# Prompt attention: VectorE's low half before the take in short tiles, early products in the last slot of their step

## What is computed

```
s = einsum('bqhd,bkhd->bhqk', q, K) * scale
s = s + F_q[..., None] - F_k
s = where(k_pos <= q_pos, s, -inf)
p = softmax(s)
o = einsum('bhqk,bkhd->bqhd', p, V)
b = o * silu(gate)
```

## Time and profile before

| what | value |
|---|---|
| median of 3 executions | 1475.28 us (1474.33 to 1477.14) |
| the profiled execution, its own time | 1475.86 us |
| its span | 1474.1 us |
| instructions | 24037 |
| PE (TensorE matmul) | 1439.7 us busy, 98% |
| DVE (VectorE) | 859.8 us, 58% |
| ACT (ScalarE) | 623.1 us, 42% |
| POOL (GpSimd) | 531.6 us, 36% |
| granted TensorE clock | 1.0 of full speed, mean |
| prompt attention, on TensorE | about 727 to 1158 us from the span's start |

### The profile page before, as it was taken

The page is one execution under the profiler, slowest core; times in us unless marked ns, Lnnn a source line. Parts: engine busy times, 40 slices in busy tenths (PEclk is TensorE's granted clock), DMA queues, the critical chain, the costliest instruction groups (busy, mean ns, idle before and its releaser), DMA issues.

```text
span 1474.1 us, 24037 instructions
## 1 busy us (share of the span) xinstructions
PE 1439.7 (98%) x8896; PEld 1299.1 (88%) x8896; DVE 859.8 (58%) x1858; ACT 623.1 (42%) x1324; POOL 531.6 (36%) x819
## 2 busy tenths in 40 slices
PE   8999999999999999999999999999999899999998
PEld 8998888888889999999988898898898799987887
DVE  4333103343355362232498898889889688798663
ACT  5434012131131110110287787788778555532220
POOL 2110003545541011010346655655655686502221
PEclk9999999999999999999999999999999999999999
DMA  5533114544232020044257536536624498635442
GB/s 166 150 126 102 46 59 129 161 129 136 87 95 62 22 72 25 12 98 94 57 97 149 110 72 140 126 64 129 132 47 138 150 329 271 235 130 185 133 160 93
DMA packets 179620, 173.95 MB, mean 118 GB/s; under 512 B 72431, under 2 KB 137872, under 8 KB 176432
## 3 DMA queue, kind: packets, MB, share of 16 engines
q1 hardware_dynamic: 176992, 163.44, 40.0%
q10 hardware_dynamic: 2448, 8.91, 1.5%
q0 software_dynamic: 64, 0.07, 0.1%
HBM read 123.27 MB, written 49.12 MB: 117 GB/s over the span
## 4 chain that ended last, share of the span: by engine, by line
PE 60%; DVE 16%; issue 11%; POOL 7%; ACT 4%; DMA 2%; SPq 0%; DVEq 0%; POOLq 0%; ACTq 0%
PE banks L1065 18%; PE banks L1059 14%; PE banks L2800 7%; DVE pa_s_ring L1589 7%; POOL in_h_rstd L586 4%; PE banks L1657 3%; POOL in_out L591 3%; PE banks L2232 3%; PE banks L1673 3%; PE banks L1674 2%; PE banks L2211 2%; PE banks L2268 2%; DVE in_out L872 2%; DVE pa_pt_lo L1618 1%; PE banks L1648 1%
## 5 line engine op out<-in xcount | busy, mean ns | idle before, releaser
L1059 PE MATMUL banks<-in_w_hi,in_xt_hi 128*128 128x512 f32 (+1 forms) x680 | 242.8, 357 | 1.5 <-ACT in_out L637 1.1
L1059 PE MATMUL banks<-in_w_hi,in_xt_lo 128*128 128x512 f32 (+1 forms) x680 | 237.8, 350 | 0.0
L1059 PE MATMUL banks<-in_w_lo,in_xt_hi 128*128 128x512 f32 (+1 forms) x680 | 237.2, 349 | 0.0
L1618 DVE TENSOR_TENSOR pa_pt_lo<-banks,pa_pt_hi 128x512 fp32r<-128x512 f32 (+2 forms) x320 | 192.7, 606 | 20.6 <-ACT pa_pt_hi L1560 19.6
L1065 PE MATMUL banks<-in_xt_hi,in_w_hi 128*128 128x384 f32 (+1 forms) x576 | 192.4, 334 | 0.9 <-DVE in_w_lo L770 0.7
L1065 PE MATMUL banks<-in_xt_hi,in_w_lo 128*128 128x384 f32 (+1 forms) x576 | 189.3, 329 | 0.0
L1065 PE MATMUL banks<-in_xt_lo,in_w_hi 128*128 128x384 f32 (+1 forms) x576 | 189.0, 328 | 0.0
L1536 ACT ACTIVATE pa_s_ring<-pa_s_ring,pa_low 128x1024 f32<-128x1024 f32 (+2 forms) x192 | 172.9, 901 | 27.4 <-DVE pa_low L1589 25.8
L1560 ACT ACTIVATE pa_pt_hi<-banks 128x512 fp32r<-128x512 f32 (+2 forms) x320 | 162.0, 530 | 51.9 <-PE banks L1657 50.1
L1657 PE MATMUL banks<-ident,pa_s_ring 128*128 128x128 f32 x1088 | 172.3, 274 | 8.1 <-DVE pa_pt_lo L1618 7.4
L1673 PE MATMUL banks<-pa_pt_hi,pa_vs 128*128 128x256 f32 x576 | 166.1, 304 | 6.4 <-DVE pa_parts L1600 6.0
(11 more groups left out here) (309 smaller groups left out, 2887.8 us busy)
## 6 DMA issues: line engine op xcount, KB each, us to landing
sa_k_c<-in_cache_k_dram SPq DMA_DIRECT2D x8, 2048.0 KB, 10.6
sa_v_c<-in_cache_v_dram SPq DMA_DIRECT2D x28, 512.0 KB, 5.3
out_dram<-in_out SPq DMA_DIRECT2D x34, 256.0 KB, 2.1
out_dram<-op_x ACTq DMA_DIRECT2D x17, 512.0 KB, 3.3
scratch_qk_t<-in_t_hi SPq DMA_DIRECT2D x32, 256.0 KB, 2.6
scratch_qk_t<-in_t_lo SPq DMA_DIRECT2D x32, 256.0 KB, 3.0
pa_q_l<-scratch_qk_t SPq DMA_DIRECT2D x16, 512.0 KB, 13.0
pa_ks<-scratch_qk_t SPq DMA_DIRECT2D x16, 512.0 KB, 6.5
```

Source lines behind the costliest of these rows:

```text
L1059: mm = pe.matmul(ps[:, u % NBANK, 0:n], tile_of(xa, t)[:, k, :], wa[:, k, c0:c0 + n], start=(k == 0 and q == 0), stop=(k == KT - 1 and q = ...
L1618: dve.tensor_tensor(pt_lo[g % 2][:, b:b + nb, cols], ps_t[:, turn_use(h, j, n) % 3, 0:nb * P].rearrange("p (b q) -> p b q", q=P), pt_hi[g ...
```

## The change

On VectorE, in steps whose tile has a single quad (j = 0 to 3), the low half of tile j now stands ahead of the take of tile j + 3's first quad. On TensorE, for 2 <= j < 8 (BLK = 8), all blocks of products of a step are multiplied in its last slot, after that slot's turn and scores, and no longer spread over the slots. Everything else is as it was.

```diff
@@ -1608,7 +1608,7 @@
                 n_take = len(quads(nxt[1])) if nxt else 0
                 slots = max(len(banks), n_take)
                 for n in range(slots):
-                    if n < n_take:
+                    if n < n_take and len(banks) > 1:
                         take_chunk(*nxt, n)
                     if n < len(banks):
                         b, nb = banks[n]
@@ -1619,6 +1619,8 @@
                                           ps_t[:, turn_use(h, j, n) % 3, 0:nb * P].rearrange("p (b q) -> p b q", q=P),
                                           pt_hi[g % 2][:, b:b + nb, cols].bitcast(F32),
                                           ALU.subtract).then_inc(lo_done, 1)
+                    if n < n_take and len(banks) == 1:
+                        take_chunk(*nxt, n)
                     if n == min(1, slots - 1) and j % 2 == 1:
                         ended = pair_ended(h, j - 1, LAG)
                         if ended:
@@ -1705,7 +1707,9 @@
                         done = pair_ended(h, j - 1, LAG)
                         if done:
                             turn_output(*done)
-                    if ended:
+                    if ended and 2 <= j < BLK:
+                        values(*ended, ours if n == slots - 1 else [])
+                    elif ended:
                         values(*ended, ours[len(ours) * n // slots:len(ours) * (n + 1) // slots])
         turn_output(H - 1, NG - 2)
         following("queries")
```

## The result

The changed kernel takes 1478.61 us (median of 20 runs, 1476.46 to 1480.34) against 1474.93 us before (median of 20). Two of the 20 executions before, 1565.61 and 3509.92 us, lie far outside the others, and the ratio leaves them out. It is 1.0022, 95% interval 1.0015 to 1.0028: slower by 0.22%, some 3.3 us (the two medians are 3.7 us apart). The interval leaves out 1, but the difference is hardly more than the 3 us that the forecast took as no change. The profiled execution took 1477.82 us, its span is 1476.1 us.

A forecast was written before the change was run, and what follows sets the result against it. VectorE, almost gapless within a head, was taken to bound the prompt attention. +0.6 us in heads 1 to 7 and +0.2 us in head 0 made +0.8 us: 1476.1 us forecast, range 1473.2 to 1478.9 us.

The forecast's parts named there:

- What bounds a head: From step 2 VectorE works almost without a gap; TensorE's waits in steps 2 to 7 are its shadow.
- Late start (a): Step 2 of heads 1 to 7 begins with tile 2's low half, waiting for ACT's high half: +0.12 us on the path.
- Neighbouring takes (b): Steps 2 and 3: second take directly behind the first, losing overlap; +0.115 us each, +0.23 us a head, bounds nothing to 0.17 each.
- the signs for right: Low half 0.12 us late, gap near 0.03 us, tile 8's wait gone, TensorE's waits shifted, head 53.2 to 53.3 us.
- (c): Step 3's low half would find its input ready and not wait, with only 0.05 us to spare.
- The take-back: Tile 8's scores end earlier, so VectorE recovers its 0.19 us wait and 0.08 us overlap: at most -0.27 us a head.
- The sum: Heads 1 to 7: 0.12 + 0.23 - 0.27 = +0.08 us each; head 0 +0.2 us; together +0.8 us.
- The case: Whole kernel: time within about 0.2%, 3 us, of no change; chance 0.83, faster 0.07, slower 0.10.
- Rival A: TensorE's waits in steps 4 and 6 are lost time and vanish: -10.4 us, 1464.9 us; chance 0.06.
- B: Neighbouring takes cost nothing; heads 1 to 7 gain 0.15 us each, 1474.2 us; chance 0.16.
- C: Postponed products hold up step 5 and tile 8's scores, nothing comes back; 0.46 us a head, 1478.9 us; chance 0.09.
- The waits forecast for TensorE: Step 4's wait shrinks below 0.6 us, step 6's goes, step 8's grows from 0.23 to about 0.9 us.

The follow-up runs named there:

- e2: Kernel before with only the products of steps 4 to 7 moved to the last slot, VectorE's order as before; 1473.12 us, ratio 0.9984.
- e7: Changed kernel with the gating of steps 1 and 3 between the two takes instead of behind them; 1475.55 us, 1.0003 of the kernel before.
- e6: e2 with ScalarE's copy of an output (even steps) behind the second high half of its step; 1464.92 us, 0.9925 of the kernel before.
- e1: Changed kernel with products spread over the slots as before, so only VectorE's order differs; 1480.51 us, 1.0036 of the kernel before.
- e3: Changed kernel where second takes of tiles 4 to 6 neither wait for nor read the first take's minimum; 1473.62 us, 0.9988 of the kernel before.
- e5: Changed kernel with the low half ahead of the first take in steps 4 to 7 too; 1484.14 us, 1.0055 of the kernel before.
- e4: Changed kernel where second takes of tiles 4 to 6 still wait but start from a constant; 1477.18 us, 1.0010 of the kernel before.

## Why the prediction was right or wrong

- **What bounds a head** held: VectorE, with ScalarE at some places, from the low half or take of step 2 to the late steps. e2 (TensorE's waits moved, 0.4 us a head and not 1.3), e7 (its wait removed, nothing gained) and e6 (VectorE's waits for ScalarE shortened, 0.95 us a head on top of e2) show it from three sides.
- **Late start (a)** held: +0.12 us, in e1 one part of 0.64.
- **Neighbouring takes (b)** is the step that failed, in size: the term of +0.23 us a head was 0.52 us. The forecast took 0.115 us each from two dependent additions with a gap of 0.03 us, and named 0.17 us as the upper bound from handoffs between engines. Measured is a gap of 0.18 us, so 0.26 us each, beyond the bound. The price was read from a pair whose second instruction carries its wait itself, while a second take has a wait instruction of its own ahead of it (0.10 us already in the pair one row higher, at 1310.83), two semaphores in it, and a read-out to wait for. e1, e3 and e5 show the price; what share of it each of the three has is read from rows alone. The line for wrong, a head over 53.5 us, was just not crossed by heads 1 and 3 to 6 (53.48 to 53.50), but the signs for right, a gap near 0.03 us and a head of 53.2 to 53.3 us, were missed.
- **(c)** held, but by luck: the low half of step 3 did not wait in the changed kernel, where the larger gap of (b) had put it at 893.34. In e3, where the takes overlap, it waited, by 0.15 us with the lost overlap. With a gap as small as the forecast's it would have had next to no margin.
- **The take-back** held as a mechanism and was somewhat larger, 0.38 for 0.27 us.
- **The sum**: 0.12 + 0.52 - 0.38 = 0.26 us a head against 0.28 measured (53.48 to 53.50 for 53.19 to 53.24), and head 0 3 x 0.26 - 0.15 = 0.63 us, measured 0.63 (49.51 for 48.88); the 0.15 us is the forecast's own estimate and was not measured apart. Seven heads, head 0 and another 0.2 us in head 2 (below) make 2.65 us of the stage's 2.71. The forecast had 0.8.
- **The case**: "within 0.2%" was taken with 0.83; the measured 0.22% is just past that line, its interval on both sides of it. The time lies in the range. Rival A fell (e2: 2 us, not 10), and B with the measured gap. C's 1478.9 us is nearer to the measured time than the forecast's 1476.1, but C got there by a way that the runs refute: the products held nothing up, the take-back came, and the neighbours alone were dear. That the time lies in the range is luck too: the neighbours at their upper price gave only 1477.0, and the rest of the range, up to 1478.9, is the 1.9 us that it allowed for the spread of the runs.
- **The waits forecast for TensorE**: step 4 under 0.6 us held (0.57), that of step 6 is gone, and step 8's growth held in kind, with 0.68 for 0.9 us. Why it fell short is open: the late gating of step 3 does not explain it, for e2, without that, has 0.69 us. "Step 4 shrinks" says little by itself, since all of step 4 together took 0.07 us more (893.55 to 896.39, for 893.48 to 896.25).
- **The Trainium skill's rule**, VectorE: DVE Perf Modes, "The DRAIN you can't avoid": a semaphore between chained operations costs nothing (it measured eight copies), which the forecast worked out as -1.0 us (its own terms give -1.2: seven heads at -0.15 us and head 0 at -0.15). The runs do not agree: e3 and e4 differ in the waits alone and by 0.38 us a head (0.52 us, less 0.15 us of a low half that then had to wait in e3).

## What to carry to other kernels

Where a busy engine sets the time, a wait on its own semaphore is hidden only by the instruction that stands between producer and consumer; moving that instruction away exposes it. Its price must be read from a pair of the same kind: whether the wait sits in the instruction or in one of its own ahead of it made 0.03 or 0.10 us here, and the takes had 0.15 to 0.18 us. A wait of TensorE that ends with another engine's instruction was worth nothing here as long as that engine had no gaps (e7): look for the gaps in that engine's own list, the ones of 0.05 to 0.2 us too, and at which instruction of a third engine they end. In e6 they lay behind a copy on ScalarE that could stand later.

## What had not been expected of the hardware

From the accumulator's read-out to the next take of the same engine it is 0.18 us (0.15 us where the second take has no diagonal quad, and so a wait for one semaphore instead of two ahead of it). Dependent additions have 0.03 us when the wait is in the instruction, and 0.10 us when it is one of its own. A take with its starting value from SBUF is 0.06 us longer than one with a constant. And in head 2, in every kernel that keeps the wait, the second take of tile 5 starts 0.35 us later than in other heads (0.54 us after the first, in the kernel before too, where all but 0.14 us of it is covered). It costs the changed kernel 0.33 us against its other heads; in e3, without the wait, it is absent. The wait instruction itself runs at its usual place there (838.98 to 839.03, behind a read-out that ends at 838.94), and the take starts only at 839.48. What makes it so in this one head was not tried and stays open.
